# One stage of a hybrid decoder layer: order of minima, output steps and copies in the merged attention and delta-rule stage

## The reference

```python
# attention, per block of 128 queries
s = (q_nope @ k_nope + q_pe @ k_pe) * scale          # S
p = softmax(where(k_pos <= q_pos, s, -inf))           # X: minimum of -s and exp
o = p @ v                                             # T (transpose p), V
y_mla = rmsnorm(o)                                    # O, A, AS
# delta rule, per chunk
a = tril(beta * (k @ k.T) * decay);  qk = tril(q @ k.T * decay)   # K, KA
v_new = inv(I + a) @ (beta * v - ... @ state)         # LB, I, IS, L, Y, WU, KS, TR
o = q @ state * exp(g) + qk @ v_new                   # QS, AV
state = state * exp(g_last) + k_dec.T @ v_new         # DS
y_gdn = rmsnorm(o) * silu(gate)                       # O1, O2
```

## Time and profile before

| | us |
|---|---|
| median of 3 runs | 2453.58 |
| lowest, highest | 2445.33, 2453.86 |
| profiled execution | 2449.63 |
| its span | 2447.9 |

### The profile page before, as it was taken

How to read it: one execution, slowest core, us unless ns; L and a number is a source line. 1 busy time by engine, 2 the same in 40 slices (tenths; PEclk the granted TensorE clock), 3 DMA queues, 4 the chain that set the end, 5 groups by cost and what they waited for, 6 DMA issues and landing times. The chain is left out here.

```text
span 2447.9 us, 35572 instructions
## 1 busy us (share of the span) xinstructions
PE 2191.6 (90%) x11478; PEld 1245.6 (51%) x11479; DVE 1034.5 (42%) x2278; ACT 835.2 (34%) x2027; POOL 646.8 (26%) x1119
## 2 busy tenths in 40 slices
PE   6999999999967898899989996999938999999990
PEld 2545454545435566666656673455534444444440
DVE  2334243333345566666577763243461222222223
ACT  2264363552744444455445561111101111111113
POOL 1100001000034533634533501332302222222224
PEclk9999999999988999999999998999968999999995
DMA  9212121122252344434244218433305788999777
GB/s 347 75 61 76 48 76 57 46 74 68 82 167 86 103 126 131 131 105 138 80 137 138 74 58 323 178 113 129 114 24 159 223 247 269 300 324 288 222 223 292
DMA packets 221897, 361.77 MB, mean 148 GB/s; under 512 B 45579, under 2 KB 143526, under 8 KB 218294
## 3 DMA queue, kind: packets, MB, share of 16 engines
q1 hardware_dynamic: 207926, 309.57, 37.2%
q0 software_dynamic: 13824, 50.34, 8.5%
HBM read 259.93 MB, written 99.93 MB: 147 GB/s over the span
## 5 line engine op out<-in xcount | busy, mean ns | idle before, releaser
L704 PE MATMUL pV<-keys_values_then_all,w_in_sb 128*128 128x512 f32 x768 | 340.1, 596 | 4.1 <-DVE keys_values_then_all L518 4.1
L2141 PE MATMUL hidden_ps<-w,keys_values_then_all 128*128 x752 | 331.5, 594 | 2.0 <-SPq L2013 2.0
L1234 ACT ACTIVATE probs<-scores,neg_max 128x512 f32<-128x512 f32 (+3 forms) x320 | 196.3, 620 | 303.4 <-DVE neg_max L1343 182.1
L2141 PEld LDWEIGHTS hidden_ps<-w,keys_values_then_all 128*128 128x128 f32 x752 | 143.2, 191 | 182.5 <-issue 182.4
L704 PEld LDWEIGHTS pV<-keys_values_then_all,w_in_sb 128*128 128x128 f32 x768 | 144.4, 191 | 177.0 <-issue 176.2
L1790 PE MATMUL out_ps<-keys_values_then_all 128*128 128x512 f32 x512 | 226.1, 600 | 2.5 <-ACT keys_values_then_all L1655 2.5
L1496 PE MATMUL scores<-ident,probs 128*128 128x128 f32 x1088 | 156.5, 286 | 38.3 <-ACT probs L1234 37.6
L2071 ACT ACTIVATE keys_values_then_all<-hidden_ps 128x256 f32<-128x256 f32 x47 | 18.0, 384 | 456.5 <-PE hidden_ps L2141 456.5
L2151 PE MATMUL expert_ps<-w_sb,keys_values_then_all 128*128 x368 | 169.8, 604 | 0.0
L1790 PEld LDWEIGHTS out_ps<-keys_values_then_all 128*128 128x128 f32 x512 | 96.9, 192 | 121.7 <-issue 116.5
L1496 PEld LDWEIGHTS scores<-ident,probs 128*128 128x128 f32 x1088 | 121.0, 144 | 67.8 <-ACT probs L1234 59.3
(11 more groups left out here) (365 smaller groups left out, 3207.9 us busy)
## 6 DMA issues: line engine op xcount, KB each, us to landing
w<-in_w_dram SPq DMA_DIRECT2D x64, 1024.0 KB, 10.8
w_sb<-in_w_dram SPq DMA_DIRECT2D x32, 1024.0 KB, 14.1
keys_values_then_all<-in_x_dram SPq DMA_DIRECT2D x32, 512.0 KB, 5.4
w_mod_rows<-in_w_mod_dram SPq DMA_DIRECT2D x16, 1024.0 KB, 4.8
keys_values_then_all<-in_w_mod_dram SPq DMA_DIRECT2D x4, 2048.0 KB, 15.1
qkv_d<-l_out SPq DMA_DIRECT2D x32, 256.0 KB, 2.3
keys_values_then_all<-y_d SPq DMA_DIRECT2D x16, 512.0 KB, 4.7
x_d<-keys_values_then_all SPq DMA_DIRECT2D x16, 512.0 KB, 2.7
```

The source lines that it names most:

```text
L704: last = pe.matmul(pV[n % 2][:], win[:, k, QKV0 + c * P:QKV0 + (c + 1) * P], hT[:, s % 2, k, :], start=(k == 0), stop=(k == ND - 1))
L1234: act.activation(prob[:, e, 0:w].rearrange("p t k -> p (t k)"), pS[e][:, 0:w * P], ACT.Exp, scale=-1.0, bias=nmin[:, i % 2, h, b:b + 1], a ...
L2141: last = pe.matmul(pH[par][:], xT[par][:, k], m.w13[:, ds(slot, 1), k].rearrange("p s n -> p (s n)"), start=(k == 0), stop=(k == ND - 1))
```

## The change

Five edits, all in `mix_order` and `mix`:

- All four X of quad j+1 follow S(j+1) directly; before, X 2 and X 3 came between V 0 and V 1 of quad j, after the chunk steps spread in there.
- Of the two output steps O that go with a quad, the first stays before S and the second moves behind V. A moves with it, behind V for every tile; AS of the small tiles moves to the next tile's first quad, behind T.
- G and O2 are held back until after the next V, or until just before the next K or QS.
- All four copies of T are on ScalarE, with one semaphore `t_copied`.
- `lt_new` and `at_new` have two buffers; SP's loads for later chunks follow the first store of chunk products (`load_next`).

```diff
@@ mix_order
-        if i and o < AH // 4:
-            for hp in (2 * o, 2 * o + 1):
-                atoms.append((0.13 * (TILE[i - 1] // 4 + 1), [("O", i - 1, hp)]))
+        if i > 1 and first and TILE[i - 1] < 4:
+            atoms.append((0.0, [("AS", i - 2, 0)]))
+        turns = [(0.13 * (TILE[i - 1] // 4 + 1), [("O", i - 1, hp)]) for hp in (2 * o, 2 * o + 1)] * (i > 0 and o < AH // 4)
+        atoms += turns[:1]
         if ahead:
-            atoms.append((0.8 * ahead, [("S", j + 1), ("X", j + 1, 0), ("X", j + 1, 1)]))
-        if i and last:
-            atoms.append((0.0, [("A", i - 1, 0)] * (TILE[i] < 4) + [("AS", i - 1, 0)]))
-        atoms.append((0.65 * n, [("V", j, 0)] + [("X", j + 1, 2), ("X", j + 1, 3)] * (ahead > 0) + [("V", j, 1)]))
-        if i and o == AH // 4 - 1 and TILE[i] >= 4:
+            atoms.append((0.8 * ahead, [("S", j + 1)] + [("X", j + 1, e) for e in range(4)]))
+        if i and last and TILE[i] >= 4:
+            atoms.append((0.0, [("AS", i - 1, 0)]))
+        atoms.append((0.65 * n, [("V", j, 0), ("V", j, 1)]))
+        atoms += turns[1:]
+        if i and o == AH // 4 - 1:
             atoms.append((0.0, [("A", i - 1, 0)]))
...
-    atoms.append((0.0, [("BX", NT - 1, 0), ("B2", NT - 1, 0)]))
+    atoms.append((0.0, [("AS", NT - 2, 0), ("BX", NT - 1, 0), ("B2", NT - 1, 0)]))
...
+    held = []
     for cost, step in steps:
+        if step[0] in ("O2", "G"):
+            held.append(step)
+            continue
+        if step[0] in ("K", "QS"):
+            order += held
+            held = []
         order.append(step)
         owed += cost * share
         while atoms and owed >= atoms[0][0]:
             owed -= atoms[0][0]
-            order += atoms.pop(0)[1]
+            order += atoms[0][1]
+            if atoms.pop(0)[1][0][0] == "V":
+                order += held
+                held = []
+    order += held
@@ mix
-        lt, lt_new, at_new = (sb(n, [P, GH, P]) for n in ("A_transposed", "A_ahead", "qk_ahead"))
+        lt = sb("A_transposed", [P, GH, P])
+        lt_new, at_new = sb("A_ahead", [P, 2, GH, P]), sb("qk_ahead", [P, 2, GH, P])
...
@@ SP: load_kk(2), load_q(1), load_gate(0), the bias pieces and load_mod(0) become load_next
                 elif kind == "KA":
                     store_products(n)
+                    if n == 0:
+                        load_next()
@@ ScalarE
-                elif kind == "T" and step[2] % 2 == 0:
+                elif kind == "T":
                     e, w = step[2], width(n)
                     wait(t_ready, 4 * n + e + 1)
                     wait(pv_ready, 2 * n + e // 2 - 1)
-                    act.copy(probT[:, e, 0:w].rearrange("p t q -> p (t q)"), pS[e][:, 0:w * P]).then_inc(t_copied[0], 1)
+                    act.copy(probT[:, e, 0:w].rearrange("p t q -> p (t q)"), pS[e][:, 0:w * P]).then_inc(t_copied, 1)
@@ VectorE: K and KA wait for the store before the last one; the copies go
-                    wait(lt_stored, 16 * n)
+                    wait(lt_stored, 16 * (n - 1))
...
-                    wait(at_stored, 16 * n)
+                    wait(at_stored, 16 * (n - 1))
...
-                elif kind == "T" and step[2] % 2 == 1:
-                    e, w = step[2], width(n)
-                    wait(t_ready, 4 * n + e + 1)
-                    wait(pv_ready, 2 * n + e // 2 - 1)
-                    dve.tensor_copy(probT[:, e, 0:w].rearrange("p t q -> p (t q)"), pS[e][:, 0:w * P]).then_inc(t_copied[1], 1)
@@ TensorE, S and V
-                    for half in range(2):
-                        wait(t_copied[half], 2 * n)
+                    wait(t_copied, 4 * n)
...
-                    for e in range(2):
-                        wait(t_copied[e], u + 1)
+                    wait(t_copied, 4 * n + 2 + 2 * step[2])
```

More of the change, by code:

```diff
@@ L924, in mix @@
         s_ready, min_ready, exp_done, t_ready = sem("s_ready"), sem("min_ready"), sem("exp_done"), sem("t_ready")
-        t_copied = [sem("t_copied0"), sem("t_copied1")]
+        t_copied = sem("t_copied")
         pv_ready, oT_copied, low_ready, gap_ready, wexp_ready, wgt_step, wgt_ready = (sem(n) for n in (
@@ L982, in store_products @@
                 wait(lt_ready, c + 1)
-                sp.dma_start(m.a_d[c * P:(c + 1) * P, :], lt_new[:].rearrange("p h i -> p (h i)")).then_inc(lt_stored, 16)
+                sp.dma_start(m.a_d[c * P:(c + 1) * P, :], lt_new[:, c % 2].rearrange("p h i -> p (h i)")).then_inc(lt_stored, 16)
                 wait(at_ready, c + 1)
-                sp.dma_start(m.qk_d[c * P:(c + 1) * P, :], at_new[:].rearrange("p h i -> p (h i)")).then_inc(at_stored, 16)
+                sp.dma_start(m.qk_d[c * P:(c + 1) * P, :], at_new[:, c % 2].rearrange("p h i -> p (h i)")).then_inc(at_stored, 16)
             def load_blocks(c):
@@ L1046, in _, with load_next @@
             load_g(1)
[L1047 to L1053, removed]
+            def load_next():
+                load_kk(2)
+                load_q(1)
+                load_gate(0)
+                sp.wait_ge(bias_zero, 1)
+                for r in range(8):
+                    sp.dma_start(mod_sum[32 * (r % 4):32 * (r % 4) + 1, r // 4], b_mod[0:1, 2 * D + r * 512:2 * D + (r + 1) * 512]
+                                 ).then_inc(bias_loaded, 16)
+                load_mod(0)
             sp.wait_ge(mask_made, 1)
@@ L1271, in _ @@
                     wait(em_ready, n + 1)
-                    wait(lt_stored, 16 * n)
+                    wait(lt_stored, 16 * (n - 1))
                     both = [bank[b] for b in at_bank[step]]
                     for h in range(GH):
-                        last = dve.scalar_tensor_tensor(out=lt_new[:, h], in0=both[h // 2][:, (h % 2) * 2], scalar=beta[:, cols(n, h)],
+                        last = dve.scalar_tensor_tensor(out=lt_new[:, n % 2, h], in0=both[h // 2][:, (h % 2) * 2], scalar=beta[:, cols(n, h)],
                                                         in1=em[:, h], op0=ALU.mult, op1=ALU.mult)
@@ L1278, in _ @@
                 elif kind == "KA":
-                    wait(at_stored, 16 * n)
+                    wait(at_stored, 16 * (n - 1))
                     both = [bank[b] for b in at_bank[("K", n)]]
                     for g in range(2):
-                        last = dve.tensor_tensor(at_new[:, g * 2:g * 2 + 2], both[g][:].rearrange("p (h two) i -> p h two i", two=2)[:, :, 1],
+                        last = dve.tensor_tensor(at_new[:, n % 2, g * 2:g * 2 + 2], both[g][:].rearrange("p (h two) i -> p h two i", two=2)[:, :, 1],
                                                  em[:, g * 2:g * 2 + 2], ALU.mult)
```

## The result

| | us |
|---|---|
| after, median | 2454.06 (2449.77 to 2458.06) |
| before, median beside it | 2448.59 (2444.39 to 2453.86) |
| ratio after / before | 1.0022, 95% interval 1.0016 to 1.0028 |

The change is no gain: 5.5 us slower. The interval leaves out 1, but this is less than the 0.5% (12 us) that the prediction calls no change. It is 34 us above the 2420 us forecast and 4 us above the end of its range, 2450. The profiled execution has a span of 2454.5 us.

What follows compares the result with a forecast made beforehand. TensorE, busy 705.11 of the merged stage's 799 us, was taken as the bound, with 94 us idle. From 2449.63, -25 + 14 - 3.9 - 5 - 12 + 1.5 = -30.4 gave 2419, stated as 2420; range 2388 to 2450, forecast's own 2397 to 2438.

Steps and rivals of the forecast that it cites:

- three signs of being wrong: S's wait past 45 us, bank waits for output products growing, or the merged stage's granted clock staying at 0.96.
- holding G: In the merged list: K waits for the decay behind all minima, with no copies behind it on VectorE; no cost in the sum.
- T's waits: At the probability transposes: minima directly behind scores remove 25 of 37.6 us waiting for exponentials; bounds 11 and 37.6.
- Four copies: At S: all four probability copies on ScalarE run one behind another and cost 14 us; bounds -9 and +31.
- Start and buffers: At the stage's start: two chunk-product buffers and later loads free the first K and second S, gaining 3.9 us; bounds 0, 5.5.
- Output split: At PSUM banks: output steps split around V seldom hold two of three banks, gaining 5 us; bounds 14.5 gained, 9 lost.
- The clock: On TensorE in the merged stage: fewer stalls bring back 12 us lost to half-clock stretches; bounds 0 and 21.
- The end: At the stage's end: the last A, AS and output step move behind V, adding 1.5 us; bounds 0 and 3.
- Rival 1: Waits only move from T to S because ScalarE's queue is the chain, no clock back: 2449 us, chance 0.14.
- Rival 3: At every quad's T copies ScalarE becomes the bound, 0.7 us in all 79 rounds: 2472 us, slower, chance 0.08.

Runs made afterwards that it cites:

- e9: The kernel before with one edit alone, G held until after the next V or just before K or QS: 2478.2 us, ratio 1.0126.
- e1: The changed kernel with G no longer held, only O2 held: 2424.85 us, ratio 0.9902 to the kernel before.
- e2: The changed kernel, G still held, with the probability copies shared again between ScalarE and VectorE: 2450.16 us, ratio 1.0007 to the kernel before.
- e4: The changed kernel with G in place and the probability copies shared again between ScalarE and VectorE: 2415.25 us, ratio 0.9863 to the kernel before.
- e5: The changed kernel, G still held on VectorE and ScalarE but at its old place in GpSimd's list: 2435.49 us, ratio 0.994 to the kernel before.
- e6: e4 with X 2 and X 3 put back between V 0 and V 1: 2422.86 us, ratio 0.9889 to the kernel before.
- e10: The kernel before with one edit alone, all four probability copies on ScalarE: 2461.62 us, ratio 1.0062.
- e8: e4 with one buffer for each chunk product and SP's loads in front of the list again: 2420.16 us, ratio 0.9884 to the kernel before.
- e7: e4 with both output steps of a quad before S again: 2429.37 us, ratio 0.9916 to the kernel before.
- e11: e4 with G moved earlier, ahead of the second Y step: 2415.79 us, ratio 0.986 to the kernel before.
- e12: e11 with both output steps of the last tile before V again: 2416.46 us, ratio 0.987 to the kernel before.

## Why the prediction was wrong

The mechanisms that the sum named were there. The step that failed is one that it costed at nothing. Of its three signs of being wrong, the clock came true (0.95 over the stage); the other two came near, S's wait with 43.8 of 45 us and the bank waits for output products with 14.2 us where they were 14.5, now in fewer and longer pieces.

- **The step that failed: holding G.** "A held step is put out before K or QS at the latest; K then waits for the decay (exp on ScalarE, product on GpSimd) behind all minima. Behind that wait on VectorE are only chunk steps and the next output step, no copies." Shown instead: 28.1 us (e9), 29.2 us (after against e1) and 34.9 (e2 against e4). Two things were not followed. GpSimd's product is named, but not its place in GpSimd's queue: there the hold moves it behind one more inversion piece of 2.88 us, so that at chunk 12 it comes 8.13 us after its input is ready, where in e1 it came 5.84 us after (1158.79 to 1164.63). And behind K on VectorE stand, besides the output product that frees a bank, the minima of the next quad (K12 S50 X50 in the list), so a late K stops T through minima and exponential. The earlier trace rows had shown this very chain at 4.59 us, and the prediction read it as a reason to move the minima, not as the price of a late decay. e5 shows the GpSimd part, about two thirds; what makes the rest stays open.
- **T's waits (-25 taken, bounds -11 and -37.6).** The waits fell as forecast, from 37.6 to 9.6, though with a piece of 7.7 us where none over 3 was forecast. But the time they were worth is 7.6 us (e6 against e4), below the lower bound. 18.7 us of waits went and 12.4 us appeared behind other resources; the prediction took waits for time.
- **Four copies (+14, bounds -9 and +31).** Measured +9.6 (e1 against e4) and +11.5 (e10), but +3.9 under the hold (after against e2). Nearly right, and a loss in all three. S's wait came out at 43.8 us, over the expected 20 to 35, just under the 45 at which the forecast was to be given up.
- **Start and buffers (-3.9, bounds 0 and -5.5).** Measured -4.9 (e8 against e4), by the mechanism named. Right; 711.29 less 707.3 is 4.0, not 3.9, which changes nothing.
- **Output split (-5, bounds -14.5 and +9).** Measured -14.1 (e7 against e4): against e7, out_parts waits fall from 21.9 to 6.2 us in e4. Mechanism right, size nearly at the bound.
- **The clock (-12).** After got 1.2 us of busy time back, since its stalls had only moved (102.2 us idle, 93.2 before). With G in place (e1) it is 9.0 us, in e4 16.7 and in e11 8.8, so the term was of the right size and hung on the stalls, though not on their sum alone.
- **The end (+1.5, bounds 0 and 3).** Some 4 us in the traces (e11 against e12), over the upper bound; in the medians nothing that can be told.

The five measured terms without the hold of G are -7.6, +9.6, -4.9, -14.1 and, for O2, -1.7: -18.7 us, where e1 as a whole measured -23.7 and the sum had -30.4. O2's share is within the noise, and each term was taken with the others in place and with its own share of the clock, so they need not add up; the 5 us between stay open. e1's 2424.85 us lies in the forecast's own range of 2397 to 2438; the 29 us from there to 2454 are the one step costed at nothing. Rival 1 gives nearly the right time (2449) for the wrong reason: e1 shows S at 41.2 us and yet 24 us faster than before. Rival 3's place is the one that e10 shows, but its 0.7 us in each of 79 rounds, 55 us, came to 11.5.

## What to carry to other kernels

When a step is moved in a list that all engines walk, follow each of its instructions into its own engine's queue, and look there for what now stands ahead of it; a product that takes 1.26 us on GpSimd cost the kernel some 28 us, two thirds of it because, chunk after chunk, a piece of 2.9 us came to stand in front of it while the consumer's queue stood still. Then look at what stands behind the consumer that will wait: here a late K held minima, banks and, through them, TensorE. And count a removed wait as time only after asking which wait ends next: of 18.7 us of waits removed, at most 7.6 us were gained.

## What the runs showed of the hardware

TensorE's busy time for the same 6624 matmuls was not the same: 688.4 us in e4, 696.1 in e1, 705.1 before, 715.2 in e9, beside idle times of 74.2, 77.4, 93.2 and 115.8 us. A stall can so be paid for beyond its own length. In after, behind the 7.72 us stand, TensorE was busy for 3.06 of the 3.10 us from 1198.90 to 1202.00 at a granted clock of 0.50, its lower level; behind the 7.76 us stand, from 913 to 918 us, at 0.55. Over the stage, e9 has 22.6 us more idle time than the kernel before and 10.1 us more busy time. The granted clock goes with it (0.98, 0.96, 0.96 and 0.94 over the stage). e11 keeps the link from being exact: its idle time is less than e4's, at 72.7 us, and its busy time is 696.3, in an execution 3.5 us above its median. The Trainium skill, "TensorE: Matmul & The Clock Gate", Part 1, says that the slow rate is the default and activity earns the fast one; these rows agree in direction, and e11 speaks against idle time alone setting it.
